# Between layers: the last and first outputs, the norm and the addition by two halves of the tokens; the squares of the norm put off, their sums on VectorE

## The chip, the cores and the metric

The kernel runs on one core of one Trainium2 chip. The metric is the device time of one execution in microseconds. Engines are named as in the profile: PE is TensorE's matmul, PEld its weight load, DVE is VectorE, ACT is ScalarE, POOL is GpSimd, SP is SyncE, which issues the transfers.

## What is computed

Two decoder blocks in fp32 over 512 tokens of width 1024. The first has two layers, the second one layer over 528 tokens (16 meta tokens in front). Around every mixer, cross-attention and feed-forward stands the same frame, and it is what the change touches:

```python
def rms_norm(x, gain):
    x32 = x.astype(jnp.float32)
    y = x32 * lax.rsqrt(jnp.mean(x32 * x32, axis=-1, keepdims=True) + RMS_EPS)
    return (y * gain.astype(jnp.float32)).astype(x.dtype)

    for layer in range(DEPTH):
        hn = rms_norm(x, g[0])
        y = mlstm_mixer(hn, ...) if layer % 2 == 0 else stick_breaking_mixer(hn, ...)
        x = x + rms_norm(y, g[1])
        y = memory_cross_attention(rms_norm(x, g[2]), mem_n, xa_w_q[layer], xa_w_kv[layer], xa_w_o[layer])
        x = x + rms_norm(y, g[3])
        y = swiglu_ffn(rms_norm(x, g[4]), ffn_w_gate_up[layer], ffn_w_down[layer])
        x = x + rms_norm(y, g[5])
```

The second block is a gated mixer (`mix`) and a feed-forward with a short convolution, in the same frame.

## The kernel before

**Layout.** Everything lies transposed: `x` is [128, 8, 528], eight strips of 128 features, tokens along the free axis. A product `h @ W` is made output by output: an output is 128 features by all tokens in a PSUM bank (512 columns; where the 528 tokens go, two banks of 264), the sum over 8 strips (22 in `down`). To keep fp32's exactness at the rate of `float32r`, every operand is split into a rounded upper part and a rest (`u_hi`, `u_lo`, `w_hi`, `w_lo`), and each tile is three matmuls (`tile`, L359): hi x hi, lo x hi, hi x lo.

**Weights** come as 384 units of 8 tiles (512 KB). SP transfers a unit to `w_land` (two places) once GpSimd is done with the unit two before, ScalarE writes `w_hi` (L777, `hi_to`) once TensorE is done with the unit four before, GpSimd writes `w_lo` (L1731, `lo_to`). A ring holds four units (`RING`). `UNIT[name]` is where the units of a product begin. `hi_to(n)` stands in ScalarE's program at fixed places, and so sets what waits behind it there.

**Between two layers** (`p` is the number of the addition, `n` = `p` + 1 that of the next norm) the engines do this, each in its own written order, with semaphores between them:
- ScalarE copies each output out of PSUM (`y_out`, L821), VectorE squares it and adds it up in `acc` (L1250, L1252).
- TensorE multiplies `acc` by ones (`y_mean`, L381), which sums over the features; ScalarE takes logarithm and exponent of it (`y_rstd`, L782, L787): the inverse root `rstd_y`.
- VectorE goes through the eight strips: `y * gain * rstd_y` (L1210), added to `x` (L1212), and, one strip later, `u_lo` (L1203). ScalarE makes `u_hi` (L796) and the square of `x` (L800) of each strip; GpSimd adds the squares up in `acc` (`x_sums`, L1740).
- TensorE's `head` takes the first outputs of the next product side by side (three, in `mix_in` two), strip by strip as `u_lo` comes, then the mean of `acc` for the next norm (`mean`, bank 6), then the other outputs one by one (`outputs`). The norm's scale `rstd` is not in `u`: VectorE multiplies it in when it takes an output out of PSUM, so an output can be made without `rstd`, but its bank is not free before it.

The banks rotate by small functions: `four` (banks 0 to 3), `six` (three pairs), `conv_banks` (0 and 1, 2, 3 and 4, 5). The norms' means use 5 and 6.

There are six such places: `xa_o0` to `up0`, `down0` to `sb_q`, `xa_o1` to `up1`, `down1` to `mix_in`, `mix_out` to `up2`, and `down2` to the end, where SP stores the strips.

ScalarE needs the table of its function; where the program names none, a load is put before the logarithm and another before the exponent.

## Time and profile before

| | us |
|---|---|
| median of 3 runs | 2699.49 (2697.83 to 2703.25) |
| the profiled execution, its own time | 2702.27 |
| its span, first to last instruction | 2700.9 |
| mean granted clock of TensorE | 0.951 |

| engine | busy us | share |
|---|---|---|
| PE | 2456.8 | 91% |
| POOL | 1064.4 | 39% |
| DVE | 982.2 | 36% |
| ACT | 897.1 | 33% |

The busy shares are an average over stages with different limits; which wait ends last in a stage is read from the chain and the waits. TensorE's clock has two levels, 1.2 and 2.4 GHz, shown as 0.5 and 1.0.

### The profile page before, as it was taken

To read this page: it belongs to the slowest core of one execution; us is meant where nothing else is said; L and a number is where in the kernel's file an instruction comes from. 1 tells how busy PE (TensorE), PEld (TensorE's weight loads), DVE (VectorE), ACT (ScalarE), POOL (GpSimd) and SP (SyncE) were. 2 spreads that over 40 slices of the span, in tenths; PEclk is the share of its full clock that TensorE was granted. 3 is DMA by queue.
4 is the path that set the end of the run, shared out by engine and by line. 5 is a ranking of instruction groups with operands and counts; after the bars stand their busy time and mean duration, and the time that the engine had idled before them with its cause. 6 is when DMAs were issued, how large, how long until landed. Compare 5 with 4: busy or idle time off the path is not lost.

```text
span 2700.9 us, 29218 instructions
## 1 busy us (share of the span) xinstructions
PE 2456.8 (91%) x12268; PEld 2017.8 (75%) x12268; DVE 982.2 (36%) x1312; ACT 897.1 (33%) x1194; POOL 1064.4 (39%) x466
## 2 busy tenths in 40 slices
PE   7986898899999798989888999997998998899997
PEld 5754775678888586668666788885988998799885
DVE  3245623422211411444423422204556442754402
ACT  4322432332222323664323322223434323322221
POOL 5321551444444442005514444444423433444442
PEclk9987998899999898999899999998989999999998
DMA  4211230122233121003312222222200222132231
GB/s 146 86 39 34 99 125 24 56 101 97 98 101 102 63 94 55 1 1 102 125 39 70 71 94 97 99 102 85 87 32 27 99 79 79 63 99 91 92 109 70
DMA packets 62850, 211.47 MB, mean 78 GB/s; under 512 B 8704, under 2 KB 10880, under 8 KB 62720
## 3 DMA queue, kind: packets, MB, share of 16 engines
q1 hardware_dynamic: 57968, 206.20, 22.8%
q10 hardware_dynamic: 4752, 3.42, 0.4%
q8 instruction: 97, 1.59, 0.2%
q14 instruction: 33, 0.27, 0.0%
HBM read 207.49 MB, written 2.10 MB: 78 GB/s over the span
## 4 chain that ended last, share of the span: by engine, by line
PE 80%; DVE 12%; ACT 4%; issue 2%; DMA 1%; POOL 0%; ACTq 0%; SPq 0%; DVEq 0%
PE ps L359 64%; PE ps L416 4%; DVE x L1212 3%; DVE u_lo L1203 2%; DVE arena L1210 2%; PE ps L544 1%; PE ps L611 1%; PE ps L651 1%; PE ps L524 1%; PE ps L481 1%; DVE y_ffn L1210 1%; PE ps L597 1%; PE ps L587 1%; PE ps L599 1%; DMA w_land<-in_units 1%
## 5 line engine op out<-in xcount | busy, mean ns | idle before, releaser
L1731 POOL TENSOR_TENSOR w_lo<-w_land,w_hi 128x1024 fp32r<-128x1024 f32 x384 | 955.1, 2489 | 1398.6 <-ACT w_hi L777 1398.2
L359 PE MATMUL ps<-u_hi,w_hi 128*128 128x512 f32 (+2 forms) x2448 | 800.1, 358 | 99.5 <-DVE u_lo L1203 62.6
L359 PE MATMUL ps<-u_lo,w_hi 128*128 128x512 f32 (+2 forms) x2448 | 797.1, 357 | 0.0
L359 PE MATMUL ps<-u_hi,w_lo 128*128 128x512 f32 (+2 forms) x2448 | 792.8, 355 | 0.0
L359 PEld LDWEIGHTS ps<-u_hi,w_hi 128*128 128x128 f32 x2448 | 437.5, 191 | 188.5 <-issue 51.5
L777 ACT ACTIVATE w_hi<-w_land 128x1024 fp32r<-128x1024 f32 x384 | 403.2, 1051 | 478.8 <-PE ps L359 350.4
L359 PEld LDWEIGHTS ps<-u_hi,w_lo 128*128 128x128 f32 x2448 | 435.3, 191 | 66.4
L359 PEld LDWEIGHTS ps<-u_lo,w_hi 128*128 128x128 f32 x2448 | 434.9, 191 | 66.0 <-issue 0.7
L359 PE MATMUL ps<-hid_hi,w_lo 128*128 128x512 f32 x528 | 208.3, 395 | 0.0
L359 PE MATMUL ps<-hid_lo,w_hi 128*128 128x512 f32 x528 | 208.3, 395 | 0.0
L359 PE MATMUL ps<-hid_hi,w_hi 128*128 128x512 f32 x528 | 208.3, 395 | 0.0
L1250 DVE TENSOR_TENSOR sq<-y_ffn 128x512 f32<-128x512 f32 x24 | 16.6, 692 | 329.7 <-ACT y_ffn L821 329.7
L1228 DVE TENSOR_TENSOR arena<-ps,rstd 128x264 f32<-128x264 f32 (+1 forms) x92 | 46.0, 530 | 247.0 <-PE ps L359 230.2
L1463 DVE TENSOR_TENSOR arena<-ps,rstd 128x512 f32<-128x512 f32 x66 | 45.6, 690 | 239.3 <-PE ps L359 239.3
L999 ACT ACTIVATE hid_hi<-arena 128x512 fp32r<-128x512 f32 x66 | 41.7, 631 | 246.6 <-DVE arena L1466 246.6
L359 PEld LDWEIGHTS ps<-hid_hi,w_lo 128*128 128x128 f32 x528 | 99.5, 188 | 23.3
L359 PEld LDWEIGHTS ps<-hid_hi,w_hi 128*128 128x128 f32 x528 | 99.5, 188 | 23.2
L359 PEld LDWEIGHTS ps<-hid_lo,w_hi 128*128 128x128 f32 x528 | 99.5, 188 | 23.1
L1740 POOL TENSOR_TENSOR acc<-acc,sq 128x512 f32<-128x512 f32 (+1 forms) x42 | 66.0, 1571 | 57.5 <-ACT sq L800 56.6
L1250 DVE TENSOR_TENSOR sq<-arena 128x512 f32<-128x512 f32 (+1 forms) x40 | 27.8, 695 | 163.4 <-ACT arena L821 163.4
L796 ACT ACTIVATE u_hi<-x,vecs 128x512 fp32r<-128x512 f32 (+1 forms) x64 | 46.3, 723 | 120.5 <-DVE x L1212 120.5
L821 ACT ACTIVATE arena<-ps 128x512 f32<-128x512 f32 (+1 forms) x48 | 24.5, 529 | 160.2 <-PE ps L359 160.2
(281 smaller groups left out, 2930.0 us busy)
## 6 DMA issues: line engine op xcount, KB each, us to landing
w_land<-in_units SPq DMA_DIRECT2D x384, 512.0 KB, 3.2
x<-in_xT SPq DMA_DIRECT2D x4, 528.0 KB, 7.1
arena<-in_memT ACTq DMA_DIRECT2D x2, 1024.0 KB, 5.2
outT<-x SPq DMA_DIRECT2D x8, 256.0 KB, 2.0
consts<-in_consts SPq DMA_DIRECT2D x1, 448.0 KB, 7.8
arena<-in_masks ACTq DMA_DIRECT2D x1, 448.0 KB, 3.4
arena<-in_consts ACTq DMA_DIRECT2D x1, 296.0 KB, 3.8
arena<-in_consts ACTq DMA_DIRECT2D x1, 256.0 KB
```

Source lines behind the costliest of these rows:

```text
L359: ins = pe.matmul(ps[:, bank, 0:c1 - c0], w, rhs(k, c0, c1)[which], start=first and h == 0, stop=last and h == 2)
L416: ins = pe.matmul(ps[:, 4 * g + b, :], a_, w_[:, u % RING, cols], start=k == 0 and n == 0, stop=k == DT - 1 and n == 2)
L777: act.activation(w_hi[:, u % RING, :], w_land[:, u % LAND, :], ACT.Copy).then_inc(*unit_hi.up())
L796: act.activation(u_hi[:, k, a:z], x[:, k, a:z], ACT.Copy, scale=col(gain, k)).then_inc(*u_hi_at.up())
L1203: dve.scalar_tensor_tensor(u_lo[:, k, a:z], x[:, k, a:z], col(gain, k), u_hi[:, k, a:z].bitcast(F32), ALU.mult, ALU.subtract).then_inc(*u_ ...
L1210: dve.scalar_tensor_tensor(y[:, k, :], y[:, k, :], col(POST[p], k), rstd_y[:, cols], ALU.mult, ALU.mult).then_inc(*dve_own.up())
L1212: dve.tensor_tensor(x[:, k, cols], x[:, k, cols], y[:, k, :], ALU.add).then_inc(*x_new.up())
L1228: ins = dve.tensor_tensor(v, p_, rstd[:, c0:c1], ALU.mult)
L1250: dve.tensor_tensor(sq[:, o % 2, 0:w], y[:, o, :], y[:, o, :], ALU.mult).then_inc(*dve_own.up())
L1463: dve.tensor_tensor(w, bank, rs, ALU.mult).then_inc(*emptied_by[name, o])
L1731: pool.tensor_tensor(w_lo[:, u % RING, :], w_land[:, u % LAND, :], w_hi[:, u % RING, :].bitcast(F32), ALU.subtract).then_inc(*unit_lo.up())
L1740: pool.tensor_tensor(acc[:, a:z], acc[:, a:z], sq[:, k % 2, a:z], ALU.add).then_inc(*x_sum.up())
```

## The change

For the six places the last outputs of a product (`LAST`: two, in the `down` products one) are made by halves of the tokens: tokens up to 256 of the last two outputs, then the rest. Mean, inverse root, addition to `x`, `u_hi` and `u_lo` and the head of the next product go by the same halves, the first half through all strips and then the second. The squares of `x` are taken on ScalarE behind all of that, for whole strips, and added up on VectorE (`x_sums` of these places goes from GpSimd). The mean of the next norm stands one output later on TensorE. `wide` gives `up0`, `up1`, `sb_q` and `sb_k` six banks. The table of logarithm and exponent is loaded ahead of the norm of `mix_out` instead of behind it. `GATE_PARTS` is cut at the same token.

```diff
+CUT = META + S // 2
+LAST = {1: 2, 2: 1, 4: 2, 5: 1, 6: 2, 7: 1}
+HALVES = [(META, CUT), (CUT, N)]
+Y_HALVES = {p: [(0 if p == 6 else META, CUT), (CUT, N)] for p in LAST}
+X_HALVES = {p + 1: [(0 if p in (5, 6) else META, CUT), (CUT, N)] for p in LAST}
...
+        wide = lambda o: [(0, 1, 2, 3, 4, 7)[o % 6]]
...
+            def last_outputs(p, name, outs, rhs, banks_of, other_bank):
+                first = DT - LAST[p]
+                for h, (c0, c1) in enumerate(Y_HALVES[p]):
+                    for o in range(first, DT):
+                        bank = other_bank[o] if h else banks_of(o)[0]
+                        await_empty([bank])
+                        tiles = outs[o]
+                        for n, (uj, q, k) in enumerate(tiles):
+                            ins = tile(UNIT[name] + uj, q, k, rhs, [(c0, c1)], [bank], n == 0, n == len(tiles) - 1)
+                            if h and (n == len(tiles) - 1 or tiles[n + 1][0] != uj):
+                                ins.then_inc(*unit_done.up())
+                            if h and o == first and n == 4:
+                                half_mean(p, 0)
+                        if h == 0:
+                            ins.then_inc(*full[bank].up())
+                        holds((name, o, h), [bank], unit_done.at(UNIT[name] + tiles[-1][0] + 1) if h else full[bank].now())
+            def half_mean(p, h):
+                pe.wait_ge(*y_sum.at(Y_SUMS[p] + 8 + (LAST[p] if h else 0)))
+                mean(("y", p, h), acc, [Y_HALVES[p][h]], 5)
+            def half_head(n, name, banks_of, abreast, part_of=None):
+                parts = part_of or (lambda o: PRE[n][1])
+                for h in range(2):
+                    for k in range(UT):
+                        pe.wait_ge(*u_lo_at.at(step(n, k, h)))
+                        for o in range(abreast):
+                            behind = 2 if o == abreast - 1 else 0
+                            for kk in range(max(k - behind, 0), k - behind + 1) if k < UT - 1 else range(k - behind, UT):
+                                if len(parts(o)) == 2:
+                                    part, bank, at = parts(o)[h], banks_of(o)[h], 0
+                                else:
+                                    c0, c1 = parts(o)[0]
+                                    part, bank, at = ((CUT, c1) if h else (c0, CUT)), banks_of(o)[0], (CUT - c0 if h else 0)
+                                if kk == 0 and (h == 0 or at == 0):
+                                    await_empty([bank])
+                                ins = tile(UNIT[name] + o, kk, kk, u_rhs, [part], [bank], kk == 0, kk == UT - 1, at)
+                            if h and k == UT - 1:
+                                ins.then_inc(*unit_done.up())
+                                holds((name, o), banks_of(o), unit_done.at(UNIT[name] + o + 1))
+                        if h == 0 and k == (3 if LAST[n - 1] == 2 else 4):
+                            half_mean(n - 1, 1)
+            def norm_mean(n):
+                pe.wait_ge(*x_sum.at(summed(n, 7)))
+                mean(("x", n), acc, PRE[n][1], 6)
...
+                    half_head(n, f"up{i}", wide, 3)
+                    outputs(f"up{i}", PAIRS, u_rhs, ONE, wide, 3, 4)
+                    norm_mean(n)
+                    outputs(f"up{i}", PAIRS, u_rhs, ONE, wide, 4)
...
+                half_head(6, "mix_in", six, 2)
+                output("mix_in", 2, PAIRS[:20], u_rhs, TWO, six(2))
+                norm_mean(6)
+                outputs("mix_in", PAIRS[:20], u_rhs, TWO, six, 3, FIRST_FILLER)
...
+            def out_and_norm(p, name, outs, y, y_parts, following, steps=None):
...
+                for o in range(first):
+                    hi_after(name, outs, o)
+                    act.wait_ge(*ready_at[name, o])
+                    for (c0, c1), b in zip(y_parts, banks_at[name, o]):
+                        ins = act.activation(y[:, o, c0 - a:c1 - a], ps[:, b, 0:c1 - c0], ACT.Copy)
+                    ins.then_inc(*emptied_by[name, o])
+                if following:
+                    hi_to(UNIT[following] + LAST[p])
+                for o in range(first, DT):
+                    copy(o, 0)
+                rsqrt_mean(("y", p, 0), [Y_HALVES[p][0]], D, rstd_y, rstd_y_at)
+                if not following:
+                    copy(DT - 1, 1)
+                    rsqrt_mean(("y", p, 1), [Y_HALVES[p][1]], D, rstd_y, rstd_y_at)
+                    return
+                if LAST[p] == 2:
+                    copy(DT - 2, 1)
+                hi_to(UNIT[following] + 1 + LAST[p])
                 for k in range(DT):
+                    upper_step(n, k)
+                    if k == 1 and LAST[p] == 1:
+                        hi_to(UNIT[following] + 3)
+                    if k == (2 if LAST[p] == 2 else 3):
+                        copy(DT - 1, 1)
+                        hi_to(UNIT[following] + 4)
+                rsqrt_mean(("y", p, 1), [Y_HALVES[p][1]], D, rstd_y, rstd_y_at)
+                for k in range(DT):
+                    upper_step(n, k, 1)
+                    if steps and k == 0:
+                        steps()
+                for k in range(DT):
+                    square_step(n, k)
...
+            def norm_end(n, name):
+                hi_to(UNIT[name] + RING + (2 if n == 6 else 3))
...
+            def out_and_norm(p, name, y, a, w, following=True):
+                first, n = DT - LAST[p], p + 1
+                dve.memset(acc[:, :], 0.0).then_inc(*dve_own.up())
+                def square(o, ready, c0, c1):
+                    dve.wait_ge(*ready)
+                    dve.tensor_tensor(sq[:, o % 2, c0:c1], y[:, o, c0 - a:c1 - a], y[:, o, c0 - a:c1 - a], ALU.mult).then_inc(*dve_own.up())
+                    own()
+                    dve.tensor_tensor(acc[:, c0:c1], acc[:, c0:c1], sq[:, o % 2, c0:c1], ALU.add).then_inc(*y_sum.up())
+                    dve.wait_ge(*y_sum.now())
+                for o in range(first):
+                    square(o, emptied_at[name, o], a, a + w)
+                for o in range(first, DT):
+                    square(o, emptied_at[name, o, 0], *Y_HALVES[p][0])
+                for h in range(2):
+                    for k in range(DT):
+                        add(p, y, k, h)
+                        if following and k:
+                            low_step(n, k - 1, h)
+                        if h == 0 and LAST[p] == 2 and k in (0, 2):
+                            square(6 + k // 2, emptied_at[name, 6 + k // 2, 1], *Y_HALVES[p][1])
+                        if h == 0 and LAST[p] == 1 and k == 3:
+                            square(7, emptied_at[name, 7, 1], *Y_HALVES[p][1])
+                    if following:
+                        low_step(n, DT - 1, h)
+                if following:
+                    c0, c1 = PRE[n][1][0][0], N
+                    for k in range(1, DT):
+                        dve.wait_ge(*x_sq.at(8 * n + k + 1))
+                        if k > 1:
+                            dve.wait_ge(*x_sum.at(summed(n, k - 1)))
+                        dve.tensor_tensor(acc[:, c0:c1], acc[:, c0:c1], sq[:, k % 2, c0:c1], ALU.add).then_inc(*x_sum.up())
...
-            lo_to(UNIT["up0"] + LEAD + 1)
-            x_sums(2)
-            lo_to(UNIT["sb_q"] + LEAD + 1)
-            x_sums(3)
```

In the built program the change reads as follows. ScalarE between `xa_o0` and `up0` before (`arena<-ps` is the copy of an output, `rstd_y` its logarithm and exponent, `acc<-x` and `sq<-x` the squares for the next norm):

```order
L777 ACTIVATE w_hi<-w_land 128x1024 [waits unit_multiplied,unit_landed0]
L821 ACTIVATE arena<-ps 128x512 [waits unit_multiplied]
L782 ACTIVATE rstd_y<-ps,eps 128x512 [waits bank5_full]
L787 ACTIVATE rstd_y<-rstd_y 128x512 [waits bank5_emptied]
L777 ACTIVATE w_hi<-w_land 128x1024 [waits unit_multiplied,unit_landed1]
L796 ACTIVATE u_hi<-x,vecs 128x512 [waits x_new]
L800 ACTIVATE acc<-x 128x512
L796 ACTIVATE u_hi<-x,vecs 128x512 [waits x_new]
```

and the same place now:

```order
L865 ACTIVATE w_hi<-w_land 128x1024 [waits unit_multiplied,unit_landed1]
L904 ACTIVATE arena<-ps 128x256 [waits bank2_full]
L904 ACTIVATE arena<-ps 128x256 [waits bank3_full]
L870 ACTIVATE rstd_y<-ps,eps 128x256 [waits bank5_full]
L875 ACTIVATE rstd_y<-rstd_y 128x256 [waits bank5_emptied]
L904 ACTIVATE arena<-ps 128x256 [waits unit_multiplied]
L865 ACTIVATE w_hi<-w_land 128x1024 [waits unit_multiplied,unit_landed0]
L888 ACTIVATE u_hi<-x,vecs 128x256 [waits x_new] x3
L904 ACTIVATE arena<-ps 128x256 [waits unit_multiplied]
L865 ACTIVATE w_hi<-w_land 128x1024 [waits unit_multiplied,unit_landed1]
L888 ACTIVATE u_hi<-x,vecs 128x256 [waits x_new] x5
L870 ACTIVATE rstd_y<-ps,eps 128x256 [waits bank5_full]
```

The copies of the second halves and the writing of two weight units stand among the `u_hi` of the first half now, and the squares are gone from between them.

GpSimd around the head of `up0` before (`acc<-acc,sq` are `x_sums`):

```order
L1731 TENSOR_TENSOR w_lo<-w_land,w_hi 128x1024 [waits unit_hi] x34
L1740 TENSOR_TENSOR acc<-acc,sq 128x512 [waits x_squared]
L1740 TENSOR_TENSOR acc<-acc,sq 128x512 [waits x_summed,x_squared] x6
L1731 TENSOR_TENSOR w_lo<-w_land,w_hi 128x1024 [waits unit_hi] x68
L1740 TENSOR_TENSOR acc<-acc,sq 128x512 [waits x_squared]
```

and VectorE at the end of that head now:

```order
L1340 SCALAR_TENSOR_TENSOR arena<-arena,vecs,rstd_y 128x256
L1342 TENSOR_TENSOR x<-x,arena 128x256 [waits dve_own]
L1330 SCALAR_TENSOR_TENSOR u_lo<-x,vecs,u_hi 128x256 [waits u_hi] x2
L1377 TENSOR_TENSOR acc<-acc,sq 128x512 [waits x_squared]
L1377 TENSOR_TENSOR acc<-acc,sq 128x512 [waits x_summed,x_squared] x6
L1604 TENSOR_TENSOR arena<-ps,rstd 128x512 [waits unit_multiplied,rstd]
```

The seven additions moved from GpSimd to VectorE, behind the last `u_lo` and ahead of the first scaling with `rstd`.

ScalarE in the middle of the boundary from `down0` to `sb_q` now, between the first and the second half:

```order
L865 ACTIVATE w_hi<-w_land 128x1024 [waits unit_multiplied,unit_landed1]
L888 ACTIVATE u_hi<-x,vecs 128x256 [waits x_new] x4
L870 ACT_TABLE_LOAD
L870 ACTIVATE rstd_y<-ps,eps 128x256 [waits bank5_full]
L875 ACT_TABLE_LOAD
L875 ACTIVATE rstd_y<-rstd_y 128x256 [waits bank5_emptied]
L888 ACTIVATE u_hi<-x,vecs 128x256 [waits x_new] x8
L895 ACTIVATE acc<-x 128x512
```

There a logarithm and an exponent, each with its load, stand where before was none; in all the boundary has six loads, before it had four.

## Rows read from the trace of the kernel before

**Rows 1.** The page, part 4: the chain that ended last, by engine

```profile
PE 80%; DVE 12%; ACT 4%; issue 2%; DMA 1%; POOL 0%; ACTq 0%; SPq 0%; DVEq 0%
```

**Rows 2.** PE's waits: waited for, us in total, times, longest

```profile
PE ps L359 <- DVE u_lo L1203: 62.6, 23, 8.7
```

**Rows 3.** PE's timeline, `xa_o0` to `up0`: start, us; idle before in brackets

```profile
505.90 1.22 PE L381 MATMUL ps<-acc,consts 128*128 128x512 f32 x2 [2.21 <-DVE acc L1252]
...
514.49 0.77 PE L359 MATMUL ps<-u_hi,w_hi 128*128 128x512 f32 x1 [7.37 <-DVE u_lo L1203]
...
545.24 0.50 PE L359 MATMUL ps<-u_hi,w_hi 128*128 128x512 f32 x1 [0.65 <-DVE arena L1447]
```

**Rows 4.** DVE's timeline, a strip and the next, same boundary

```profile
513.48 0.75 DVE L1203 SCALAR_TENSOR_TENSOR u_lo<-x,vecs,u_hi 128x512 fp32r<-128x512 f32 x1
514.15 0.75 DVE L1210 SCALAR_TENSOR_TENSOR arena<-arena,vecs,rstd_y 128x512 f32<-128x512 f32 x1
514.93 0.69 DVE L1212 TENSOR_TENSOR x<-x,arena 128x512 f32<-128x512 f32 x1
515.54 1.77 DVE L1203 SCALAR_TENSOR_TENSOR u_lo<-x,vecs,u_hi 128x512 fp32r<-128x512 f32 x1
```

**Rows 5.** POOL's timeline, same boundary

```profile
509.53 2.76 POOL L1731 TENSOR_TENSOR w_lo<-w_land,w_hi 128x1024 fp32r<-128x1024 f32 x1 [6.98 <-ACT w_hi L777]
...
514.92 1.83 POOL L1740 TENSOR_TENSOR acc<-acc,sq 128x512 f32<-128x512 f32 x1 [2.63 <-ACT sq L800]
```

**Rows 6.** Groups by line and form: count, busy us, mean ns

```profile
L1323 DVE SCALAR_TENSOR_TENSOR arena<-arena,uT,zrow 128x256 f32<-128x256 f32 x4 | 1.9, 478 | 0.0
...
L928 ACT ACTIVATE m_hi<-arena,vecs 128x256 fp32r<-128x256 f32 x16 | 8.0, 501 | 0.0
```

**Rows 7.** The chain by time: 24 matmuls of 256 columns, 192 of 512

```profile
302.20 2.86 PE ps L359 x24
...
365.44 44.50 PE ps L359 x192
```

**Rows 8.** Busy time by stretch: PE, PEld, DVE, ACT, POOL; granted clock, DMA

```profile
514.00:520.00 6.00, 5.51 (x13) 4.38 (x14) 5.93 (x7) 2.33 (x5) 3.30 (x2) 0.50 0.16 66
...
526.00:538.00 12.00, 8.95 (x36) 6.72 (x37) 7.42 (x8) 5.77 (x8) 6.06 (x4) 1.00 0.01 2
...
936.00:940.00 4.00, 3.89 (x11) 3.05 (x12) 1.85 (x4) 0.28 (x1) 2.38 (x1) 0.61 0.23 73
```

**Rows 9.** PE's timeline at the other boundaries

```profile
892.81 1.13 PE L381 MATMUL ps<-acc,consts 128*128 128x512 f32 x2 [2.21 <-DVE acc L1252]
...
936.11 0.50 PE L359 MATMUL ps<-u_hi,w_hi 128*128 128x512 f32 x1 [3.37 <-DVE arena L1230]
...
1471.88 1.23 PE L381 MATMUL ps<-acc,consts 128*128 128x512 f32 x2 [2.21 <-DVE acc L1252]
...
1513.54 0.51 PE L359 MATMUL ps<-u_hi,w_hi 128*128 128x512 f32 x1 [0.77 <-DVE arena L1447]
...
1861.13 1.37 PE L381 MATMUL ps<-acc,consts 128*128 128x512 f32 x2 [2.21 <-DVE acc L1252]
...
2288.71 2.13 PE L381 MATMUL ps<-acc,consts 128*128 128x264 f32 x4 [2.32 <-DVE acc L1252]
...
2331.58 0.48 PE L359 MATMUL ps<-u_hi,w_hi 128*128 128x258 f32 x2 [0.91 <-DVE arena L1451]
```

**Rows 10.** The chain by time: `mix_in` from its output 2

```profile
1894.76 58.73 PE ps L359 x480
```

**Rows 11.** ACT's timeline, `down0` to `sb_q`

```profile
894.68 1.28 ACT L787 ACT_TABLE_LOAD   x1
895.97 0.63 ACT L787 ACTIVATE rstd_y<-rstd_y 128x512 f32<-128x512 f32 x1
```

**Rows 12.** PE's and DVE's timelines at the end of the program

```profile
2683.63 1.25 PE L381 MATMUL ps<-acc,consts 128*128 128x512 f32 x2 [2.21 <-DVE acc L1252]
...
2698.15 0.69 DVE L1212 TENSOR_TENSOR x<-x,y_ffn 128x512 f32<-128x512 f32 x1
```

More of the change, by code:

```diff
@@ L139 @@
 GW = N - G0
[L140 removed]
+GATE_PARTS = [(G0, META + S // 2), (META + S // 2, N)]
 AT = (0, 512, 1024, 896)
@@ L348, in await_empty, with tile @@
                         pe.wait_ge(*holder[b])
-            def tile(u, q, k, rhs, parts, banks, first, last):
+            def tile(u, q, k, rhs, parts, banks, first, last, at=0):
                 if u > begun[0]:
@@ L1720, in vector_engine @@
             ffn(2)
-            for k in range(DT):
-                add(7, y_ffn, k)
         def gpsimd_engine():
```

167 lines of the change are left out of this document (83 added, 84 removed).

## The prediction, made before the changed kernel was run

> **What bounds the kernel now.** I read the chain that ended last first, then TensorE's waits, then the timelines at the six places that the change touches. The chain is TensorE for 80% and VectorE for 12% [rows 1], so time can come only from places where TensorE stands. The largest group of its waits is for `u_lo`, 62.6 us in 23 waits [rows 2]; all of them lie at the boundaries between layers. The first boundary (`xa_o0` to `up0`) shows the pattern [rows 3]: the last output ends at 505.90 - 2.21 = 503.69, TensorE multiplies the sum of squares at 505.90, then stands 7.4 us until 514.49, works through the head at VectorE's pace, and begins output 4 of `up0` only at 545.24, after a wait for the scaling with `rstd`. Call the end of the last output E: boundary 1 lasts 41.6 us from E to output 4. The same two moments at the others [rows 9, 10]: `xa_o1` 1469.7 and 1513.5 (43.9), `down0` 890.6 and 936.1 (45.5), `mix_out` 2286.4 and 2331.6 (45.2); for `down1` output 3 of `mix_in` begins 48 of 480 matmuls after 1894.76, at 1894.76 + 48 x 0.122 = 1900.6, and E is 1858.9 (41.7). At the end E is 2681.4 and the last addition ends at 2698.84 (17.4) [rows 12].
>
> **Prices.** VectorE's step for one strip at full width is `u_lo`, product, addition: the starts lie 0.67, 0.78 and 0.61 us apart, 2.06 in all [rows 4]. The fourth of those rows takes 1.77 instead of 0.75: it ends at 517.31, 0.56 after GpSimd's sum that began at 514.92 ended (516.75) [rows 4, 5]. So a VectorE operation with two inputs in SBUF waits out a GpSimd operation that runs. For half a width the nearest row is 0.478 us against 0.75 [rows 4, 6], 0.27 less for each of three operations: 1.25 us a strip. The bounds are 1.03 (exactly half) and 2.06 (no saving); I take 1.25, since the row is of the same kind and size. ScalarE at half width takes at most 0.50 [rows 6]. TensorE: 24 matmuls of 256 columns take 2.86 us, 0.119 each, and 192 of 512 take 44.50, 0.232 each [rows 7]. So an output in halves costs 48 x 0.119 - 24 x 0.232 = 0.15 us more, one of 66 matmuls 0.4.
>
> **Boundary 1 worked through (`xa_o0`, also `xa_o1`).** The last two outputs begin at E - 11.1. Their first halves end at E - 5.4. Copy, square, addition (0.4 + 0.9) are ready before TensorE comes to the mean, 15 matmuls into the third half, at E - 3.6; mean 0.6, logarithm and exponent 0.9: the first addition starts at E - 2.1, where before not even the mean came before E + 2.2 [rows 3]. TensorE is done with all halves at E + 0.9, later than before by two times 0.15 and the mean, which the first half of the norm covers. First half on VectorE: 8 x 1.25 = 10.0, two squares of the second half 1.8, and what two `w_lo` of GpSimd hold up (2.4 to 2.8 each, [rows 5], less what they overlap) about 4.8: the last addition ends at E + 14.5. Here the removed work shows: GpSimd's seven `x_sums`, of which four or five held up a step before, are gone from this stretch, but the two weight units that were split during the outputs now fall into it. Then the last `u_hi`, logarithm and exponent, 1.4: E + 15.9. Second half, nothing on GpSimd: 8 x 1.25, the first `u_lo` behind the second addition and the last behind `u_hi`, 10.8 in all: last `u_lo` at E + 26.7. TensorE then has 5 tiles left (1.8) and the tile in work: E + 28.9; output 3, 5.6: E + 34.5. The squares that were put off (ScalarE 8 x 0.6, VectorE 7 x 0.73 behind the last `u_lo`) end at E + 32.6, under output 3, and cost nothing; without that cover they would cost 5.9. Mean 0.9: output 4 at E + 35.4. It needs no `rstd`, since `wide` has six banks. `rstd` comes at E + 40.9, bank 0 is wanted at E + 46.6. **Gain 41.6 - 35.4 = 6.1, and 43.9 - 35.4 = 8.5 for `xa_o1`.**
>
> **`down0`.** One output in halves; `rstd_y` at E - 2.9. The first half meets three weight units on GpSimd instead of two, and each ScalarE pair of logarithm and exponent needs two table loads of 1.28 [rows 11], six in place of four. The first two are partly under work, the middle two lie open: 2.6 us between the halves. Output 4 at E + 38.5. Gain 7.0. In before the wait at 936.11 also lowered the clock to 0.61 over 4 us [rows 8], 1.6 us; that goes too. **8.6.** The trace shows the exponent 0.01 us behind its load [rows 11]. The Trainium skill (ScalarE: Activation LUTs, What ACT_TABLE_LOAD costs) counts another 1.38 us of drain with every switch; an estimate by it takes 2.8 us off each of the two `down` boundaries. The rows show no such drain.
>
> **`down1` to `mix_in`.** The same up to the last `u_lo` (E + 29.8). But `mix_in` keeps six banks for three outputs, two each, so output 3 needs `rstd`. Before, `rstd` came in time: the 480 matmuls from 1894.76 stand in one piece [rows 10]. Now the sums begin only behind the last `u_lo`; the chain is 5.9 of sums, output 2 (TensorE reaches the mean at + 7.7), mean 0.9, a load, 0.85, a load, 0.64, scaling 0.85: output 3 at E + 43.1. **Loss 1.5.**
>
> **`mix_out` to `up2`.** The explicit table load now stands ahead, so none is in the chain. Last `u_lo` at E + 26.5. `conv_banks` gives output 4 the banks of output 0, so it needs `rstd`; ScalarE splits three units first, the third of which waits for its transfer: `rstd` at E + 40.9, output 4 at E + 41.8. **Gain 3.4** of the 7 by which the norm itself is earlier.
>
> **End.** First half of output 7 done at E - 7.5, `rstd_y` at E - 2.8 (two loads), eight strips of 0.85 in which the second half's square waits for the copy at E + 1.4, second half from E + 5.9: last addition E + 12.7 against E + 17.4. **Gain 4.7**; sixteen stores in place of eight go out under it.
>
> **Clock.** After the 7.4 us wait TensorE ran at 0.50 (1.2 GHz) for 6 us [rows 8], hidden under VectorE. Now the shorter strips (9 matmuls, 1.1 us at full and 2.0 at half clock) meet a supply every 1.25 us, so a slow first half runs over: bounds 0 and 3.1 us at each `xa` boundary, 1.0 taken; 0.5 at `down0`. Behind the two waits for `rstd` (4.7 and 6.6 us) the clock falls as at 936.11: 1.8 each. Together 6.1.
>
> **Sum:** 6.1 + 8.5 + 8.6 - 1.5 + 3.4 + 4.7 - 6.1 = 23.7 us. The profiled execution took 2702.3 (its span 2700.9), which gives 2678.6; the median of the runs is 2.8 below it, so 2699.5 - 23.7 = 2675.8, say 2676.
>
> **Rivals.** (a) The clock stays up, or the GpSimd units slip between strips: no clock loss and about 2 more, gain 30 to 32, 2668. For it: the wait that opens the head is 2 to 3 us in place of 7.4. Chance 0.14. (b) The first halves and the first quarter of the second ones run at 1.2 GHz: each `xa` boundary gives 1.8 and 4.1, `down0` 5.9, `mix_out` 2.6; with the end, the wait that goes at 936 and the losses at `mix_in` and behind the `rstd` waits, gain 15, 2685. Chance 0.16. (c) The half steps cost 1.5 instead of 1.25, fixed costs of the waits between ScalarE and VectorE: 16 strips x 0.25 x 5 boundaries = 20 less, gain 4, 2695. Against it: in rows 4 no gap is left between operations. Chance 0.05. (d) **Slower**: TensorE is kept at 1.2 GHz through both halves. A strip of nine matmuls then takes 2.0 against 1.25, and the head ends 10.4 us later than E + 28.9: the boundaries give -4.3, -1.9, +1.4, -2.5, -3.5, with 4.7 at the end and 4 more behind the waits: -10, 2710. It turns into a loss when about six of eight strips of the second half are slow. For it: each wait at a boundary did start a slow stretch [rows 8]; against it: from 526 to 538 TensorE was busy 8.95 of 12 us, waiting strip by strip, at a clock of 1.00 [rows 8]. The Trainium skill (TensorE: Matmul & The Clock Gate, HAM oscillation) describes just this, short pieces of work between waits that start slow every time. Chance 0.04. (e) A table switch costs twice its load of 1.28: four open loads at the two `down` boundaries, 5.1 less, 2681. The drain that the Trainium skill counts would be such a cost. Chance 0.03, since rows 11 speak against it. That the change does not do what it says is ruled out by its order of instructions. The forecast itself (gain 18 to 29) has 0.58.
>
> **Numbers.** 2676. The range 2667 to 2690 takes in (a), (b), (e) and the bounds of the clock term, and leaves out (c), (d) and the far tail of (b), 0.15 to 0.2. A measurement of this kernel can tell about 0.2%, 5.4 us, from no change. Faster by more 0.89 (forecast, a, b, e less a little), within it 0.06 (c and part of b), slower 0.05 (d and what I do not see).
>
> **What the profile of the changed kernel would show.** TensorE's first wait at a boundary 2 to 3 us instead of 7.4; VectorE's steps about 1.25 us without GpSimd, longer only beside `w_lo`; a gap of about 3 us between the halves at the `down` boundaries; output 4 of `up0` and `sb_q` without a wait, but waits of 4 to 7 us for `rstd` at output 3 of `mix_in` and output 4 of `up2`, there longer than before. I am wrong if half strips take much over 1.25, if TensorE is slow through the second halves, or if the sums behind the last `u_lo` outlast output 3.

## The result, and the profile after

The changed kernel takes 2666.12 us (median of 4 runs, 2664.14 to 2668.18) against 2701.37 (4 runs, 2697.83 to 2703.28): ratio 0.9871, interval 0.9854 to 0.9888. The forecast was 2676 with 2667 as the lower end of its range; the gain is 35 us where 24 were forecast. The profiled executions took 2702.27 and 2664.14, their spans are 2700.9 and 2662.8: 38.1 us apart.

TensorE's waits in the changed kernel (waited for, us, times, longest), against [rows 2]; the chain by engine hardly changed (TensorE 81%, VectorE 12%):

```profile
PE ps L387 <- DVE u_lo L1330: 34.2, 22, 3.1
```

The waits for `u_lo` are 28 us shorter in sum, and the longest is 3.1 instead of 8.7.

TensorE's timeline at the first boundary, `xa_o0` to `up0`, against [rows 3]:

```profile
500.05 0.59 PE L409 MATMUL ps<-acc,consts 128*128 128x256 f32 x2
...
506.86 0.46 PE L387 MATMUL ps<-u_hi,w_hi 128*128 128x256 f32 x1 [2.35 <-DVE u_lo L1330]
...
512.85 0.58 PE L387 MATMUL ps<-u_hi,w_hi 128*128 128x256 f32 x1 [3.08 <-DVE u_lo L1330]
...
537.04 1.02 PE L409 MATMUL ps<-acc,consts 128*128 128x512 f32 x2
```

The mean of the first half stands inside the outputs, the first wait is 2.35 instead of 7.37, and output 4 follows the mean of the next norm without a wait. The mean ends at 538.06, which I take as the start of output 4 wherever it needs no wait; before, output 4 began at 545.24. VectorE at the same place, against [rows 4]:

```profile
501.70 0.48 DVE L1340 SCALAR_TENSOR_TENSOR arena<-arena,vecs,rstd_y 128x256 f32<-128x256 f32 x1 [1.86 <-ACT rstd_y L875]
...
503.48 2.47 DVE L1340 SCALAR_TENSOR_TENSOR arena<-arena,vecs,rstd_y 128x256 f32<-128x256 f32 x1
...
509.95 2.44 DVE L1342 TENSOR_TENSOR x<-x,arena 128x256 f32<-128x256 f32 x1
...
514.47 0.42 DVE L1342 TENSOR_TENSOR x<-x,arena 128x256 f32<-128x256 f32 x1
514.81 0.48 DVE L1330 SCALAR_TENSOR_TENSOR u_lo<-x,vecs,u_hi 128x256 fp32r<-128x256 f32 x1
515.21 0.48 DVE L1340 SCALAR_TENSOR_TENSOR arena<-arena,vecs,rstd_y 128x256 f32<-128x256 f32 x1
515.72 0.43 DVE L1342 TENSOR_TENSOR x<-x,arena 128x256 f32<-128x256 f32 x1
...
528.68 0.48 DVE L1330 SCALAR_TENSOR_TENSOR u_lo<-x,vecs,u_hi 128x256 fp32r<-128x256 f32 x1 [0.18 <-ACT u_hi L888]
529.72 5.47 DVE L1377 TENSOR_TENSOR acc<-acc,sq 128x512 f32<-128x512 f32 x7 [0.56 <-ACT sq L895]
```

A step at half width lasts 1.25 us (from one addition at 514.47 to the next at 515.72), as taken. The two operations of 2.4 us wait out a `w_lo` of GpSimd (503.12 to 505.67 and 509.50 to 512.11): 2.47 and 2.44 instead of 0.48 and 0.42, 2.0 us each. The sums that were put off take 5.5 us under output 3 and end before TensorE wants them.

**All six boundaries.** To compare kernels I take the time from E, the end of the last output, to output 4 of the next product (output 3 in `mix_in`; the span's end for the last). In a kernel with halves no output ends at E; there E is the moment at which whole outputs would have ended: the first half's mean starts 3.64 us ahead of it with two halved outputs (48 whole matmuls of 0.232 less 63 half ones of 0.119), 5.67 with one, 3.9 in `mix_out`. The forecast is the one without its clock term.

| boundary | before | forecast | changed | sums alone | halves, GpSimd sums | four banks |
|---|---|---|---|---|---|---|
| `xa_o0` to `up0` | 41.6 | 35.4 | 34.4 | 36.9 | 40.5 | 40.4 |
| `down0` to `sb_q` | 45.5 | 38.5 | 37.7 | 37.7 | 43.8 | 46.4 |
| `xa_o1` to `up1` | 43.9 | 35.4 | 34.4 | 36.9 | 40.5 | 40.4 |
| `down1` to `mix_in` | 41.7 | 43.1 | 42.3 | 38.6 | 50.0 | 42.3 |
| `mix_out` to `up2` | 45.1 | 41.8 | 41.1 | 41.0 | 43.7 | 41.2 |
| end | 19.5 | 14.8 | 14.4 | 19.4 | 14.4 | 14.4 |
| sum | 237.3 | 209.0 | 204.2 | 210.6 | 232.9 | 225.1 |

The boundaries give 33.1 us. About 2 of them, at `xa_o1`, belong to this one execution of the kernel before: there the last two `u_lo` took 3.45 us together, beside two sums of GpSimd, where they take 1.63 at `xa_o0`, and behind TensorE's wait for them (2.48 us) the granted clock was 0.72 over 6 us. The run below that changes the old kernel only in `mix_in` has the same program at this place and lasts 41.9, not 43.9. The forecast took the 43.9 as it stood. The other 5.0 come from the six stages between them, whose own work is unchanged but for the cut of the gate outputs:

| stage, from output 4 to the next E | before | changed | again | sums alone | whole downs | named table | best |
|---|---|---|---|---|---|---|---|
| start to `xa_o0` | 503.7 | 503.7 | 504.0 | 504.1 | 509.0 | 509.3 | 503.5 |
| `up0`, `down0` | 345.3 | 345.0 | 345.0 | 345.1 | 345.1 | 345.1 | 345.0 |
| `sb_q` to `xa_o1` | 533.5 | 532.0 | 532.1 | 532.8 | 532.0 | 532.6 | 532.0 |
| `up1`, `down1` | 345.4 | 345.0 | 345.0 | 345.1 | 345.1 | 345.1 | 345.1 |
| `mix_in` to `mix_out` | 385.9 | 383.0 | 382.9 | 385.5 | 384.2 | 387.3 | 382.6 |
| `up2`, `down2` | 349.8 | 350.0 | 350.0 | 349.8 | 350.9 | 350.8 | 349.7 |

Where the sequence of work between the boundaries is the same, the first stage and the one of the mixer differ by 5 us all the same. The runs below show that the granted clock differs there.

### The profile page after: what moved, and what is told of

Same layout as the page of the kernel before. It is cut to its first block, busy times and chain, and to the rows that moved or that the text cites. A ratio compares the mean times of both kernels' runs of the same rounds, so it can differ in the third digit from the quotient of the medians.

```text
span 2662.8 us, 30534 instructions
## 1 busy us (share of the span) xinstructions
PE 2458.0 (92%) x12812; PEld 2050.3 (77%) x12812; DVE 1018.1 (38%) x1501; ACT 918.6 (34%) x1256; POOL 1009.0 (38%) x431
## 4 chain that ended last, share of the span: by engine, by line
PE 81%; DVE 12%; ACT 5%; issue 2%; DMA 0%; POOL 0%; ACTq 0%; SPq 0%; DVEq 0%
PE ps L387 65%; PE ps L494 4%; DVE x L1342 3%; PE ps L622 1%; DVE arena L1340 1%; PE ps L697 1%; PE ps L602 1%; PE ps L559 1%; PE ps L673 1%; DVE y_ffn L1340 1%; DVE u_lo L1330 1%; PE ps L683 1%; PE ps L737 1%; PE ps L685 1%; PE ps L771 0%
## 5 line engine op out<-in xcount | busy, mean ns | idle before, releaser
L387 PE MATMUL ps<-u_hi,w_hi 128*128 128x512 f32 (+3 forms) x2560 | 831.2, 351 | 76.9 <-DVE u_lo L1330 34.2
L387 PE MATMUL ps<-u_lo,w_hi 128*128 128x512 f32 (+3 forms) x2560 | 826.1, 349 | 0.0
L387 PE MATMUL ps<-u_hi,w_lo 128*128 128x512 f32 (+3 forms) x2560 | 822.4, 348 | 0.0
L387 PE MATMUL ps<-hid_hi,w_hi 128*128 128x512 f32 (+1 forms) x594 | 220.2, 371 | 0.0
L387 PE MATMUL ps<-hid_lo,w_hi 128*128 128x512 f32 (+1 forms) x594 | 219.7, 370 | 0.0
L387 PE MATMUL ps<-hid_hi,w_lo 128*128 128x512 f32 (+1 forms) x594 | 219.4, 369 | 0.0
L1620 DVE TENSOR_TENSOR arena<-ps,rstd 128x512 f32<-128x512 f32 x66 | 45.5, 690 | 229.2 <-PE ps L387 229.2
L1130 ACT ACTIVATE hid_hi<-arena 128x512 fp32r<-128x512 f32 x66 | 41.7, 632 | 234.8 <-DVE arena L1623 234.8
L888 ACT ACTIVATE u_hi<-x,vecs 128x256 fp32r<-128x256 f32 (+2 forms) x104 | 58.1, 558 | 131.6 <-DVE x L1342 131.3
L1604 DVE TENSOR_TENSOR arena<-ps,rstd 128x512 f32<-128x512 f32 x44 | 30.4, 690 | 111.7 <-PE ps L387 95.6
L1625 DVE TENSOR_TENSOR hid_lo<-arena,hid_hi 128x512 fp32r<-128x512 f32 x66 | 53.4, 809 | 46.1 <-ACT hid_hi L1130 46.1
L1330 DVE SCALAR_TENSOR_TENSOR u_lo<-x,vecs,u_hi 128x256 fp32r<-128x256 f32 (+2 forms) x104 | 64.5, 626 | 11.1 <-ACT u_hi L888 10.8
```

What stands on the lines that cost most here:

```text
L387: ins = pe.matmul(ps[:, bank, at:at + c1 - c0], w, rhs(k, c0, c1)[which], start=first and h == 0, stop=last and h == 2)
L888: act.activation(u_hi[:, k, a:z], x[:, k, a:z], ACT.Copy, scale=col(gain, k)).then_inc(*u_hi_at.up())
L1130: act.activation(hid_hi[:, f_, :], tmp[:, 2 * (f_ % 2) + 1, 0:S], ACT.Copy).then_inc(*hid_hi_at.up())
L1330: dve.scalar_tensor_tensor(u_lo[:, k, a:z], x[:, k, a:z], col(gain, k), u_hi[:, k, a:z].bitcast(F32), ALU.mult, ALU.subtract).then_inc(*u_ ...
L1620: dve.tensor_tensor(w, bank, rs, ALU.mult).then_inc(*emptied_by[name, o])
L1625: dve.tensor_tensor(hid_lo[:, f_, :], w, hid_hi[:, f_, :].bitcast(F32), ALU.subtract).then_inc(*hid_lo_at.up())
```

## The experiments

**Sums alone.** The kernel before, squares put off, their sums on VectorE, the mean one output later, six banks; nothing is halved.

```diff
+                if n in (0, 1, 4):
+                    square_step(n, k)
...
+                for k in range(DT):
+                    square_step(n, k)
...
                 low_step(n, DT - 1)
+                sums(n)
...
-            x_sums(2)
-            x_sums(3)
```

> The kernel before with one part of the change alone: squares for the next norm put off behind the last u_lo and added up on VectorE, mean one output later, six banks. No output and no strip is halved. My account (each GpSimd operation holds a two-input VectorE operation up for 1.0 us, 4 or 5 of them a boundary): last u_lo of xa_o0 to up0 at about E + 25 instead of E + 29, output 4 at E + 35.6 instead of E + 41.6; the four inner boundaries with six banks gain 5 to 8 each, mix_in and up2 about 0 because output 3 and 4 wait for rstd, the end nothing: 2680, 18 to 22 us under the kernel before. Rival (the halves bring the gain, the sums are only made room for): under 6 us, 2695 or more.

Measured: 2675.69 us, ratio 0.9900 (0.9884 to 0.9917), 26 us under the kernel before. VectorE at the first boundary, in the kernel before and then in this one:

```profile
517.23 1.77 DVE L1210 SCALAR_TENSOR_TENSOR arena<-arena,vecs,rstd_y 128x512 f32<-128x512 f32 x1
```

```profile
510.44 2.83 DVE L1233 SCALAR_TENSOR_TENSOR arena<-arena,vecs,rstd_y 128x512 f32<-128x512 f32 x1
...
523.56 0.69 DVE L1235 TENSOR_TENSOR x<-x,arena 128x512 f32<-128x512 f32 x1
524.17 0.74 DVE L1226 SCALAR_TENSOR_TENSOR u_lo<-x,vecs,u_hi 128x512 fp32r<-128x512 f32 x1
524.83 0.74 DVE L1233 SCALAR_TENSOR_TENSOR arena<-arena,vecs,rstd_y 128x512 f32<-128x512 f32 x1
525.61 0.69 DVE L1235 TENSOR_TENSOR x<-x,arena 128x512 f32<-128x512 f32 x1
526.22 1.63 DVE L1226 SCALAR_TENSOR_TENSOR u_lo<-x,vecs,u_hi 128x512 fp32r<-128x512 f32 x2
```

Before, six operations of this boundary, the one shown and the one of [rows 4] among them, took 1.77 to 1.79 us beside a sum of GpSimd: 1.0 us too long each. Here one hold by `w_lo` (2.83 us) is left; every later step takes 2.05 us, and the last two `u_lo` end at 527.9, E + 23.7, against E + 29.9 before. The 6.2 us between are the six holds, so that the squares were also put off on ScalarE needs no share of its own. 26.7 of the 33.1 us that the boundaries give are this part, and at `down0` and `mix_out` it is all. The halves add 2.5 us at each `xa_o`, nothing at `down0` and `mix_out`, 5.0 at the end, and take 3.7 away at `down1`. The account holds, its rival falls; I had expected a little less of it (18 to 22), and nothing at `mix_in` and `up2`, where the run gives 3.1 and 4.1 us.

**The halves with the sums on GpSimd.**

```diff
                     upper_step(n, k, 1)
+                    square_step(n, k)
...
-                        dve.tensor_tensor(acc[:, c0:c1], acc[:, c0:c1], sq[:, k % 2, c0:c1], ALU.add).then_inc(*x_sum.up())
...
+            lo_to(UNIT["up0"] + LEAD + 1)
+            x_sums(2)
```

> The changed kernel with its squares not put off: ScalarE squares each strip behind its second u_hi, GpSimd adds the squares up during the second half. The halves stay. My account: in the second half a GpSimd sum of 1.8 us stands beside most strips and holds VectorE up by 1 to 1.4 us each, 7 times, so the last u_lo comes 6 to 8 us later, and output 4 by 4 to 6 at the five inner boundaries: 2686 to 2694. Rival (halves bring the gain, VectorE's holds don't matter): 2666 to 2670.

Measured: 2693.63, ratio 0.9963 (0.9948 to 0.9978). GpSimd and VectorE in the second half of the first boundary:

```profile
526.49 3.01 POOL L1882 TENSOR_TENSOR acc<-acc,sq 128x512 f32<-128x512 f32 x2 [9.69 <-ACT sq L895]
```

```profile
526.85 1.52 DVE L1339 SCALAR_TENSOR_TENSOR arena<-arena,vecs,rstd_y 128x256 f32<-128x256 f32 x1
528.41 1.38 DVE L1341 TENSOR_TENSOR x<-x,arena 128x256 f32<-128x256 f32 x1
...
530.95 1.53 DVE L1329 SCALAR_TENSOR_TENSOR u_lo<-x,vecs,u_hi 128x256 fp32r<-128x256 f32 x1
```

Each sum of GpSimd makes one VectorE operation 1.0 us longer (1.52 instead of 0.48). The boundaries sum to 232.9: of the 33 us 4.4 are left, less than the end gives by itself (5.1). Between the layers, halving without freeing GpSimd is worth nothing in sum (218.5 us against 217.8).

**Four banks.**

```diff
-        wide = lambda o: [(0, 1, 2, 3, 4, 7)[o % 6]]
+        wide = lambda o: [o % 4]
```

> The changed kernel with four banks instead of six in up0, up1, sb_q and sb_k. My account: output 4 then needs the bank of output 0, which VectorE empties only with rstd, at about E + 40 instead of E + 34.4; 5.5 us at each of three boundaries and up to 1.8 more each for the clock that falls behind the wait: 2683 to 2688. Rival (TensorE's stand is only moved, the squares' sums are late anyway): under 5 us, 2671.

Measured: 2696.08 (8 runs), ratio 0.9980 (0.9970 to 0.9991): 30 us over the changed kernel, more than I had given. TensorE at output 4 of `up0` and of `sb_q`:

```profile
545.32 0.80 PE L387 MATMUL ps<-u_hi,w_hi 128*128 128x512 f32 x1 [5.99 <-DVE arena L1604]
...
938.68 0.79 PE L387 MATMUL ps<-u_hi,w_hi 128*128 128x512 f32 x1 [8.74 <-DVE arena L1387]
```

The waits for `rstd` cost 6.0, 8.7 and 6.0. Behind them the clock was low (first matmuls of 0.80 and 0.79 us, a granted clock of 0.66 from 545 to 551): the stages with `up0` and `up1` last 347.0 and 347.1 instead of 345.0. That is 24.8; the rest lies in stages that this edit doesn't touch (the first 504.9, the mixer's 388.6). So the six banks, which my sum had only named as the reason why output 4 needs no `rstd`, carry 25 of the 38 us between the two profiles: put-off sums without them would be late.

**The kernel before with TensorE 3.5 us later in `mix_in`.**

```diff
+                    if name == ("x", 6):
+                        for _ in range(4):
+                            pe.matmul(ps[:, bank + b, 0:c1 - c0], ones, sum_[:, c0:c1], start=True, stop=True)
```

> The kernel before with TensorE made 3.5 us later at one place: the two means of mix_in's norm are multiplied five times instead of once, with the same result. What it tests: between output 3 of mix_in and the last output of mix_out the changed kernel was 2.9 us shorter although nothing is changed there, and its clock stood at 1.00 from 1952 on where the kernel before ran at 0.50 for 13 us from 1975. If the clock there hangs on when the stage begins and not on the change, the slow stretch comes out different (shorter or longer by some us) in this kernel with the old order: 2698 to 2708, with that stage's own duration changed by over 1 us. If the change itself causes it, the stage lasts what it lasted, and the time is 3.5 us over the kernel before, 2704.

Measured: 2707.44 (10 runs), ratio 1.0015 (1.0002 to 1.0028). From the end of `down1` to the end of `mix_out` it takes 427.7 us against 427.5 of the kernel before, though 3.5 were added. Busy time by stretch (PE, PEld, DVE, ACT, POOL; clock, DMA), the same work in three kernels; before, changed, and this one:

```profile
1976.00:1988.00 12.00, 11.88 (x54) 11.89 (x55) 8.84 (x8) 5.10 (x10) 3.15 (x2) 0.50 0.00 1
```

```profile
1952.00:1964.00 12.00, 11.76 (x98) 11.56 (x99) 11.79 (x11) 5.34 (x11) 4.47 (x3) 1.00 0.01 1
```

```profile
1985.00:1997.00 12.00, 11.68 (x97) 11.47 (x98) 11.79 (x11) 5.30 (x10) 4.48 (x3) 1.00 0.00 0
```

In 12 us TensorE issued 54 matmuls at 1.2 GHz in the first and 98 and 97 at 2.4 GHz in the others. The kernel with the old order has the clock of the changed one here. The stage with `sb_q`, ahead of the edit, came out 2.9 us longer meanwhile (536.4), and `xa_o1` to `up1` 2.0 shorter (41.9). So in these places the clock falls out one way or the other with the order of the boundaries unchanged.

**The changed kernel again.**

> The changed kernel once more, word for word. Between the boundaries lie six stages that the change leaves alone (start to the end of xa_o0; up0 with down0; sb_q to xa_o1; up1 with down1; mix_in to mix_out; up2 with down2). In the profiled run of the changed kernel they sum to 5.1 us less than in the one of before. If that is the scatter of single executions (the clock of a stage falls out one way or the other), the boundaries last the same to 0.3 us here (34.4, 37.7, 34.4, 42.3, 41.1, 14.4) while one or two of the stages, the first or the ones with sb and mix, differ by over 1 us: 2662 to 2670. If the change causes it, all the stages last the same to 0.5 us.

Measured: 2667.58 (4 runs), ratio 0.9877 (0.9857 to 0.9896). All six boundaries agree to 0.1 us; the stages too, to 0.3, which I had expected to differ. Yet the next two kernels, with the same program up to `xa_o0`, needed 5 us more for the first stage. Two stretches of it, in the changed kernel and in the next:

```profile
20.00:40.00 20.00, 17.72 (x75) 13.75 (x74) 5.65 (x5) 7.71 (x9) 12.89 (x7) 1.00 0.33 94
160.00:180.00 20.00, 19.73 (x49) 9.99 (x48) 12.79 (x25) 6.49 (x9) 0.00 (x0) 0.74 0.06 23
```

```profile
20.00:40.00 20.00, 17.13 (x65) 12.88 (x64) 5.84 (x5) 7.44 (x9) 12.97 (x7) 0.91 0.34 86
160.00:180.00 20.00, 19.73 (x42) 9.49 (x41) 9.45 (x16) 6.20 (x8) 0.14 (x1) 0.66 0.08 26
```

TensorE's clock was lower in both (0.91 against 1.00, 0.66 against 0.74), with 65 against 75 and 42 against 49 matmuls issued. The second stretch is the one that tells: in all twelve profiles a clock of 0.74 there goes with a first stage of 503.5 to 504.9 us and one of 0.66 with 506.6 to 509.3. What decides it stays open.

**`down0` and `down1` whole.** `LAST = {1: 2, 4: 2, 6: 2, 7: 1}`; for the two products the outputs, norm and addition of the kernel before, squares and sums put off.

> The changed kernel with the outputs, the norm and the addition of down0 and down1 whole again, the squares still put off and summed on VectorE; xa_o0, xa_o1, mix_out and the end stay in halves. By the run with the sums alone, down0 to sb_q lasts 37.7 us either way and down1 to mix_in 38.6 whole against 42.3 in halves (a half boundary has the logarithm and exponent with their two table loads in its middle and ends its last u_lo later): 3.7 us less, 2662. Rival (the halves help at these two as they do at xa_o, what the run with the sums alone showed there was chance): 2666 to 2672.

Measured: 2666.98, ratio 0.9875 (0.9856 to 0.9894). `down0` 37.6, `down1` 39.1 instead of 42.3, all boundaries 201.0: 3.2 us less, as expected, while the median is the same within its interval; in the profiled execution the first stage took 5 us more. A few runs don't resolve 3 us in this kernel; the boundaries in the trace do.

**The table named ahead of the down products**, on top of that:

```diff
+                table("natural_log_exp_and_others")
                 out_and_norm(p, f"down{i}", DOWN, y_ffn, ONE, (
```

> The kernel with down0 and down1 whole, and the table of logarithm and exponent named ahead of the outputs of each down product. It takes the load of 1.28 us between logarithm and exponent out of the chain: once at down0 to sb_q (36.4), twice at down1 to mix_in (36.0, rstd_y and rstd): 3.9 us under the kernel with whole downs, 2658. If the load had a drain beside its 1.28 us, 1.28 to 1.4 more each, the gain is 8 us, 2654. At the end nothing, the second half's chain has no load in it.

Measured: 2664.90, ratio 0.9870 (0.9850 to 0.9889). `down1` to `mix_in` 36.4 instead of 39.1 (two loads of 1.28 in the chain: 2.7), `down0` 36.9 instead of 37.6, less than one load. The boundaries give 3.4 of the 3.9 us expected, and nothing beyond the loads themselves; the median is 7 us over the expectation, which had not counted the longer first stage (509.3).

**The inverse root of `mix_in` and `up2` ahead of weight units.**

```diff
-                hi_to(UNIT[name] + RING + (2 if n == 6 else 3))
+                hi_to(UNIT[name] + RING + (1 if n in (6, 7) else 3))
                 rsqrt_mean(("x", n), PRE[n][1], D, rstd, rstd_at)
+                hi_to(UNIT[name] + RING + (2 if n == 6 else 3))
```

> The same with ScalarE's inverse root of the norm moved ahead of weight units at mix_in (one unit behind it) and up2 (two units behind it, of which one waits for its transfer until 4 us after the mean). Expected: rstd of up2 4.0 us sooner, mix_out to up2 37.1 instead of 41.1, mix_in unchanged since there the mean comes last: 2654. Rival (the weight units are then late, output 4 or 5 of up2 waits for w_lo): gain under 2 us, 2656 to 2658.

Measured: 2660.71, ratio 0.9854 (0.9829 to 0.9879). ScalarE and TensorE at `up2`:

```profile
2292.40 0.93 ACT L875 ACTIVATE rstd<-ps,eps 128x264 f32<-128x264 f32 x2 [2.36 <-PE ps L409]
2293.41 0.64 ACT L880 ACTIVATE rstd<-rstd 128x528 f32<-128x528 f32 x1
```

```profile
2294.95 0.47 PE L387 MATMUL ps<-u_hi,w_hi 128*128 128x260 f32 x2 [2.15 <-DVE arena L1639]
```

The logarithm now waits for the mean alone, output 4 waits 2.15 instead of 6.33, and the boundary lasts 36.8 instead of 40.9: 4.1 us, as expected. No wait for `w_lo` stands in this place. The median is again 7 us over the expectation.

**`down0` in halves again, with the table named.** `LAST = {1: 2, 2: 1, 4: 2, 6: 2, 7: 1}`.

> The kernel with the table named ahead, the inverse root first and down1 whole, but with the last output of down0 in halves again. In the changed kernel the half boundary of down0 had a load of 1.28 us ahead of its first addition and two of them open between the halves; with the table named none is left: down0 to sb_q 37.7 - 2.6 = 35.1 against 36.9 whole, the other boundaries as in the run before (34.4, 34.4, 36.7, 36.8, 14.4). Boundaries in all 1.8 us less, 2659. Rival (VectorE's three holds by w_lo set the end of the halves and not the loads): 37 or more.

Measured: **2651.94** us (4 runs), ratio 0.9811 (0.9796 to 0.9826), the fastest of all, 14 us under the changed kernel and clear of its interval. `down0` to `sb_q` lasts 34.2, 3.5 less than in the changed kernel; all boundaries 191.0, 13.2 less. Against the run before, the median is 8.8 less but the boundaries only 2.4; in the profiles most of the rest is the mixer's stage (382.6 against 388.4), where the clock differs between executions. ScalarE between the halves of `down0`, against 3.04 us of waiting with two loads in the changed kernel (shown below):

```profile
896.79 0.47 ACT L875 ACTIVATE rstd_y<-ps,eps 128x256 f32<-128x256 f32 x1 [0.34 <-PE ps L409]
897.30 0.42 ACT L880 ACTIVATE rstd_y<-rstd_y 128x256 f32<-128x256 f32 x1
```

**The fourth weight unit behind the second half**, on top of that, at `xa_o` and `mix_out`.

```diff
                         copy(DT - 1, 1)
-                        hi_to(UNIT[following] + 4)
+                        if LAST[p] == 1:
+                            hi_to(UNIT[following] + 4)
...
+                hi_to(UNIT[following] + 4)
                 for k in range(DT):
                     square_step(n, k)
```

> The same, and at xa_o0, xa_o1 and mix_out the weight unit that ScalarE splits in the middle of the first half (the fourth of the next product) moved behind the last u_hi of the second half. The hold of 2.0 us that its w_lo puts on VectorE in the first half goes; the unit is then ready 1.05 + 2.5 us after the last u_hi, about 1.2 us after TensorE wants it for output 3. Expected: xa_o to up 33.0 to 33.3 instead of 34.4 (gain 1.1 to 1.4 at each of two), mix_out to up2 0 to 1.3 less: 2656. Rival (TensorE's own 24 head tiles, not VectorE, set the end of the head, so a hold costs nothing and the late unit costs 1.2): 35.5.

Measured: 2654.54 (5 runs), ratio 0.9816 (0.9802 to 0.9830). TensorE at output 3 and at output 4 of `up0`:

```profile
533.59 0.47 PE L387 MATMUL ps<-u_hi,w_hi 128*128 128x512 f32 x1 [0.57 <-POOL w_lo L1914]
539.23 1.02 PE L409 MATMUL ps<-acc,consts 128*128 128x512 f32 x2
541.38 0.47 PE L387 MATMUL ps<-u_hi,w_hi 128*128 128x512 f32 x1 [1.13 <-POOL w_lo L1914]
```

The mean comes 1.2 us sooner after E (32.2 against 33.4), and output 4 then waits 1.1 us for the next unit, which is late too: 34.3, no gain. At `mix_out`, where `rstd` comes last, 35.5 instead of 36.8. So at `xa_o` half of the account held: the hold did cost 1.2 us, the unit behind it costs as much.

These two runs also show what a slow clock can cost between the halves. At `down0` their programs are the same, and yet it lasts 34.2 in the one and 35.1 in the other. The six us around the second half's mean, in the run before and in this one:

```profile
894.85:900.85 6.00, 6.00 (x49) 5.95 (x48) 4.90 (x13) 2.79 (x7) 0.00 (x0) 0.94 0.01 4
899.63:905.63 6.00, 6.00 (x39) 5.82 (x38) 4.02 (x11) 2.62 (x6) 0.00 (x0) 0.74 0.02 4
```

At 0.74 the mean comes 0.5 us later after E and takes 1.05 instead of 0.59, and VectorE waits 1.70 for `rstd_y` instead of 0.78: 0.9 us.

## Why the prediction was off, point by point

The time lies 0.9 us under the range, and the gain is 11 us over the forecast. Three terms of the sum were wrong: the clock inside the halves, priced at 2.5 us, cost nothing; the boundaries were taken 4.9 us too long; the cut of the gate outputs, worth 1.7, was left out. The rest is the scatter of stages that the change leaves alone.

**The account of the boundaries held, its sizes were a little long.** First addition at E - 2.0 (2.1 forecast), last addition of the first half at E + 13.7 (14.5), last `u_lo` done at E + 25.5 (26.7), output 4 at E + 34.4 (35.4). A half step costs 1.25, rival (c) is out. The 0.8 us in the first half are the holds: 2.0 each, 4.0 in all, where I took 4.8. With that and the steps in the second half each inner boundary was 0.7 to 1.0 shorter than forecast, 4.3 us in all. The prediction's reading that four or five sums of GpSimd held up a step is short of the trace, which has six at this boundary; the sum for the halves did not use it.

**The down boundaries** behaved as told. ScalarE and VectorE between the halves of `down0` in the changed kernel:

```profile
897.92 1.28 ACT L870 ACT_TABLE_LOAD   x1
899.22 0.48 ACT L870 ACTIVATE rstd_y<-ps,eps 128x256 f32<-128x256 f32 x1
899.71 1.28 ACT L875 ACT_TABLE_LOAD   x1
901.01 0.42 ACT L875 ACTIVATE rstd_y<-rstd_y 128x256 f32<-128x256 f32 x1
```

```profile
901.46 0.49 DVE L1340 SCALAR_TENSOR_TENSOR y_ffn<-y_ffn,vecs,rstd_y 128x256 f32<-128x256 f32 x1 [3.04 <-ACT rstd_y L875]
```

Two open loads, 3.04 us of VectorE's wait, 0.01 to 0.02 us from load to function. The first load begins at 897.92, 0.01 us behind the end of a `u_hi`. Rival (e) is out: with the three loads gone (one ahead of the first addition, two here, 3.84 us by their rows) the boundary was 3.5 shorter. The Trainium skill (ScalarE: Activation LUTs, What ACT_TABLE_LOAD costs) adds 1.38 us of drain to each switch. The trace has no room for it, neither ahead of the load nor behind it.

**The waits for `rstd`** came as forecast, at output 3 of `mix_in` and output 4 of `up2`, with the clock behind them:

```profile
1874.36 0.78 PE L387 MATMUL ps<-u_hi,w_hi 128*128 128x264 f32 x2 [4.92 <-DVE arena L1385]
...
2298.39 0.77 PE L387 MATMUL ps<-u_hi,w_hi 128*128 128x260 f32 x2 [6.47 <-DVE arena L1608]
```

```profile
1874.00:1878.00 4.00, 3.64 (x16) 3.67 (x17) 1.62 (x5) 0.98 (x1) 2.36 (x1) 0.50 0.37 129
2298.00:2302.00 4.00, 3.61 (x17) 3.64 (x18) 3.63 (x6) 1.49 (x3) 0.44 (x1) 0.50 0.42 134
```

Behind them the clock cost 2.2 us (11 pairs of matmuls at 0.44 us instead of 0.24) and 1.9 (the first gate output 7.6 instead of 5.7); 1.8 each was taken. The end is exact: the last addition ends at 2661.07, E + 12.7.

**The term that failed is the clock inside the halves**, 1.0 us at each `xa_o` and 0.5 at `down0`. The slow stretch was there:

```profile
506.00:512.00 6.00, 2.90 (x12) 2.59 (x12) 5.41 (x9) 2.23 (x4) 2.50 (x1) 0.59 0.26 89
512.00:517.00 5.00, 4.15 (x19) 4.16 (x20) 4.86 (x13) 2.03 (x4) 0.11 (x1) 0.50 0.32 110
1455.86:1461.86 6.00, 2.92 (x13) 2.63 (x13) 5.41 (x9) 2.25 (x5) 2.61 (x1) 0.72 0.21 78
1461.86:1467.86 6.00, 6.00 (x35) 5.82 (x36) 5.36 (x14) 2.88 (x7) 0.00 (x0) 0.72 0.26 87
```

At `xa_o0` TensorE ran at 0.50 to 0.59 over these 11 us, at `xa_o1` at 0.72 over 12, and both boundaries last 34.4 us; in both VectorE waits 0.33 us for the second `rstd_y`. TensorE fell behind in the first half and caught up in the second, where its strip takes 1.1 us and VectorE's 1.25; I had charged what runs over out of the first half without giving the second one back. At `down0` of the changed kernel the slow mean (898.07 to 899.12) ends while ScalarE is still at its table load (until 899.20), so it is hidden too. It is not free in general: with that load gone, the last two runs differ by 0.9 us there.

Rivals (b) and (d) fall: the first halves were slow as (b) said, but the `xa` boundaries gave 7.2 and 9.5 where (b) had 1.8 and 4.1, and the second halves were not slow. The prediction also doesn't show how (d)'s figures for the other boundaries follow from its 10.4 us. Rival (a)'s 2668 is close by luck: it wants all of the clock term back, and 4.1 us of it were lost behind the waits for `rstd`; most of what made that good is the clock in the mixer's stage.

**What the sum left out.** The change also moves the cut of the gate outputs of `up2` from 258 and 258 columns to 260 and 256. I had passed over it. Starts of the next output, before and after, behind gate outputs that began at 2354.33 and 2322.83:

```profile
2360.12 0.40 PE L359 MATMUL ps<-u_hi,w_hi 128*128 128x512 f32 x1
```

```profile
2328.54 0.40 PE L387 MATMUL ps<-u_hi,w_hi 128*128 128x512 f32 x1
```

5.79 against 5.71 us, 0.08 for each of 20 gate outputs, 1.6 to 1.7 in all. It hides the clock's loss behind the wait at `up2` (350.0 against 349.8 for the stage).

**Where the whole difference lies.** The profiled gain of 38.1 against 23.7: boundaries 4.9 better than their terms (33.1 against 28.2), the clock inside them 2.5, the cut 1.7, the stages with `up0` and `up1` 0.7 (not followed up), the waits' clock 0.5 worse, and 5.1 in the mixer's stage, whose clock stood at 2.4 GHz over 12 us where it had been at 1.2; together 14.4. The last is not the change's doing as far as the runs show. Without it the gain is 33.0. Taken off 2699.5, as the forecast was, that gives 2666.5, still 0.5 us under the range: its lower end allowed a gain of 32.5, though (a) alone reached 32, and left nothing for the stages that the change leaves alone, which move the time by 5 us either way. In the medians, 35 us, part of this is averaged out.

**What I did not see** is how the gain is made up. The prediction led with the halves; the run with the sums alone shows that four fifths come from taking seven additions off GpSimd, with the six banks that let output 4 go ahead of `rstd`, and that at `down1` the halves cost 3.7 us. The parts of it were in the text (holds of 1.0 us, four or five of them; `rstd` late at `mix_in`), but I priced the change as a whole and never one part without the other.
